# Expert layers: the up matrices of the following pair are issued on ScalarE's own DMA queue instead of SyncE's

## What is computed

```python
SEQ, D_MODEL, N_EXPERTS, TOP_K, D_EXPERT = 256, 1024, 32, 2, 512

def expert_block(args):
    xblk, e = args
    hid = jax.nn.silu(xblk @ w_gate[e]) * (xblk @ w_up[e])
    return hid @ w_down[e]

...
y = jnp.zeros((t, d), xf.dtype).at[sorted_tok].add(contrib)
```

## Time and profile before

| | us |
|---|---|
| median of 3 runs | 2021.74 (2020.07 to 2021.87) |
| profiled execution, its own time | 2024.92 |
| profiled execution, span of the profile | 2023.1 |
| TensorE busy in the span | 1887.4 |
| ScalarE busy in the span | 330.8 |

### The profile page before, as it was taken

How to read it: one execution, slowest core, us unless ns; L and a number is a source line. 1 busy time by engine, 2 the same in 40 slices (tenths; PEclk the granted TensorE clock), 3 DMA queues, 4 the chain that set the end, 5 groups by cost and what they waited for, 6 DMA issues and landing times.

```text
span 2023.1 us, 21197 instructions
## 1 busy us (share of the span) xinstructions
PE 1887.4 (93%) x8074; PEld 958.2 (47%) x8074; DVE 855.9 (42%) x1552; ACT 330.8 (16%) x783; POOL 87.5 (4%) x129
## 2 busy tenths in 40 slices
PE   8999999999999999999999999989999988988886
PEld 4555665455556645855334333333874323332322
DVE  1576898833778887854111111112224111111112
ACT  2452111133521112022001000001002100000000
POOL 4102000001020002000000000000000000000000
PEclk9999999999999999999999999999999999999999
DMA  9315887651168877467999999999346999999995
GB/s 305 96 58 166 308 289 271 235 173 42 58 235 293 294 277 250 135 233 270 365 425 428 428 428 427 428 426 402 130 186 236 417 428 428 428 428 428 427 426 216
DMA packets 149242, 603.14 MB, mean 298 GB/s; under 512 B 16584, under 2 KB 60536, under 8 KB 121232
## 3 DMA queue, kind: packets, MB, share of 16 engines
q1 hardware_dynamic: 144064, 591.43, 74.2%
q0 software_dynamic: 4880, 10.22, 2.0%
q10 hardware_dynamic: 192, 0.05, 0.0%
HBM read 597.67 MB, written 1.10 MB: 296 GB/s over the span
## 4 chain that ended last, share of the span: by engine, by line
PE 63%; DMA 25%; DVE 6%; issue 2%; ACT 2%; DVEq 1%; ACTq 1%; SPq 1%
PE ps L2520 14%; DMA ring<-in_e_w_gate 13%; PE ps L935 12%; DMA ring<-in_e_w_up 11%; PE ps L638 7%; PE ps L1018 5%; PE ps L2350 4%; PE ps L2538 3%; PE ps L2282 3%; PE ps L2365 3%; PE ps L737 2%; PE ps L2464 1%; PE ps L2449 1%; ACTq L1133 1%; DMA ring<-in_e_w_down 1%
## 5 line engine op out<-in xcount | busy, mean ns | idle before, releaser
L2520 PE MATMUL ps<-ring,hT 128*64 128x512 f32 (+1 forms) x1056 | 236.8, 600 | 35.5 <-DMA ring<-in_e_w_gate 17.8
L2538 PE MATMUL ps<-ring,qkT 128*64 128x512 f32 (+1 forms) x1024 | 226.6, 594 | 10.3 <-ACT qkT L2752 8.1
L2520 PE MATMUL ps<-ring,late 128*32 128x512 f32 (+1 forms) x928 | 210.8, 608 | 26.6 <-DMA ring<-in_e_w_up 13.1
L638 PE MATMUL ps<-ring,hT 128*128 128x512 f32 (+1 forms) x384 | 172.0, 593 | 2.7 <-DMA ring<-in_w_in 1.8
L2520 PEld LDWEIGHTS ps<-ring,hT 128*64 128x64 f32 (+1 forms) x1056 | 76.4, 125 | 192.3 <-issue 192.3
L3021 DVE TENSOR_TENSOR qkT<-ps,qkT 128x512 f32<-128x512 f32 (+1 forms) x64 | 44.2, 690 | 256.0 <-PE ps L2538 256.0
L3044 DVE TENSOR_TENSOR qkT<-ps,qkT 128x512 f32<-128x512 f32 (+1 forms) x32 | 22.1, 690 | 299.9 <-PE ps L2520 299.9
L2520 PEld LDWEIGHTS ps<-ring,late 128*32 128x32 f32 (+1 forms) x928 | 68.2, 125 | 164.6 <-issue 164.6
L2538 PEld LDWEIGHTS ps<-ring,qkT 128*64 128x64 f32 (+1 forms) x1024 | 70.9, 123 | 146.5 <-issue 146.5
L1641 DVE SCALAR_TENSOR_TENSOR qkT<-ring,cc,qkT 128x512 f32<-128x512 f32 x168 | 125.8, 749 | 8.6 <-issue 0.4
L3040 DVE TENSOR_TENSOR x<-ps,x 128x1024 f32<-128x1024 f32 x22 | 26.9, 1225 | 193.9 <-PE ps L2449 193.9
(11 more groups left out here) (438 smaller groups left out, 2220.5 us busy)
## 6 DMA issues: line engine op xcount, KB each, us to landing
ring<-in_e_w_down SPq DMA_DIRECT2D x64, 2048.0 KB, 17.0
ring<-in_e_w_up SPq DMA_DIRECT2D x64, 2048.0 KB, 17.3
ring<-in_e_w_gate SPq DMA_DIRECT2D x60, 2048.0 KB, 17.2
ring<-in_ada_w SPq DMA_DIRECT2D x24, 2048.0 KB, 14.0
ring<-in_w_gate SPq DMA_DIRECT2D x16, 1408.0 KB, 8.2
ring<-in_w_up SPq DMA_DIRECT2D x16, 1408.0 KB, 8.6
ring<-in_w_down SPq DMA_DIRECT2D x22, 1024.0 KB, 5.0
ring<-in_w_in SPq DMA_DIRECT2D x8, 2048.0 KB, 11.5
```

What stands on the lines that cost most here:

```text
L638: last = mm(m.ps[:, 4 + i, 0:chunk_width(n)], m.hT[:, j, i * P:(i + 1) * P], w[:, j, :], start=(j == 0), stop=(j == KC - 1))
L2520: last = mm(dst, xg[:, j, at + x * n_tok:at + x * n_tok + place], w(x, j), start=(j == 0), stop=(j == KC - 1))
L2538: lasts[x] = mm(dst, m.hidT[:, j, rows + x * place:rows + (x + 1) * place], half_of(w(x, j), n), start=(j == 0), stop=(j == 3))
```

## The change

SyncE no longer issues the up matrices of the pairs 1 to 15. ScalarE does so, in pair p for pair p + 1, behind the silu and the first share of gather copies and ahead of the wait for the transposes. It waits for the same uses of the same slots as SyncE did. The sizes, slots and semaphores of the loads are what they were, and `second_scalar` now gets the arrays. Pair 0 (and, in further rounds, the up matrices of pair 0) stays with SyncE.

```diff
         def pairs(r):
 
-            pair(r, 1, 1, range(2, N_SLOTS), False)
+            pair(r, 1, 1, (DOWN, DOWN + 1), False)
             with sp.Fori(2, N_PAIRS - 1) as p:
-                pair(r, p, 2, range(N_SLOTS), False)
-            pair(r, N_PAIRS - 1, 2, range(N_SLOTS), True)
+                pair(r, p, 2, (GATE, GATE + 1, DOWN, DOWN + 1), False)
+            pair(r, N_PAIRS - 1, 2, (GATE, GATE + 1, DOWN, DOWN + 1), True)
...
-def second_scalar(nc, act, m):
+def second_scalar(nc, act, m, arrays):
...
                 act.wait_ge(m.e_used[slot_of(p, GATE + 1)], uses_before(r, p, GATE + 1) + 2)
                 a(m.sgx[rows], m.ps[rows, 2, :], ACT.Silu).then_inc(t["esilu"], 1)
                 gathered_next(q, 2 * h)
+                if p + 1 < N_PAIRS:
+                    for f in (UP, UP + 1):
+                        slot = slot_of(p + 1, f)
+                        act.wait_ge(m.e_used[slot], uses_before(r, p + 1, f) + 1)
+                        expert_load(act, m, arrays, l, p + 1, f, by_halves(p + 1), slot).then_inc(m.e_full[slot], 16)
                 act.wait_ge(t["hidT_ps"], it + 1)
```

More of the change, by code:

```diff
@@ L3156, in _ @@
             first_scalar(nc, act, m)
-            second_scalar(nc, act, m)
+            second_scalar(nc, act, m, a)
         @block.tensor
```

## The result

| | before | changed |
|---|---|---|
| median, us | 2021.06 (the runs beside the changed kernel's) | 2059.92 of 4 runs (2056.36 to 2062.72) |
| ratio, 95% | | 1.0189 [1.0174, 1.0204] |
| profiled execution, own time, us | 2024.92 | 2060.24 |
| span, us | 2023.1 | 2058.4 |
| TensorE, ScalarE busy, us | 1887.4, 330.8 | 1897.7, 332.2 |

The changed kernel is slower by 38.9 us, where 19 were forecast: the sign was right, the size half, and 2059.9 lies above the range (2026 to 2055). A stage is counted from its first gate matmul to the end of its last down matmul. The two stages are 36.3 us longer, the rest of the span 1.0 shorter; so all of it lies there. The two profiled executions are 35.3 us apart and not 38.9, because the one of before stood 3.9 us above its median.

The account below looks back on a forecast made before the run. The prediction took the expert layers to be bound by DMA bytes at 428 GB/s; late start 6.9, dry queue 6.0 and stage ends 6 summed to 18.9 us over the 2021.7 us median, forecast 2041 us, range 2026 to 2055.

Parts of the forecast that it names:

- issue time: ScalarE's issuing of up loads, 1.0 us a pair, is hidden or absorbed by load waits: 0, at most 4 us.
- A: Start of expert layer 1: the first up load waits behind the gather copy, so the load stream starts late: +6.9 us.
- B: Expert layer 1, one lap after the start: up lands late and the DMA queue runs dry: +6.0 us.
- A and B, layer 0: Expert layer 0: the late start only eats an existing DMA pause: 0, at most 3 us.
- middle: Middle of both expert layers: bytes unchanged, engines never dry, a pair still costs 29.4 us: 0.
- C: End of each expert layer: up of pair 15 delays gate, leaving TensorE more after the last landing: +3.3, together +6 us.
- By age after all: Rival: hardware serves both queues' loads in order of issue, so little changes: +5.6, 2027 us; chance 0.14.
- equal turns: DMA engines alternate between the two queues, sharing equally for loads with equal rows, rather than serving by age.
- This is just inside 29.4, so 0, but with no room: Expert layer 0, middle: one up-slot lap of 28.9 us fits the 29.4 us pair, so no cost.
- the up slot becomes the bound: Rival: up-slot laps are stretched by TensorE's fallen clock with the queue dry: 12 us more, 2053 us; chance 0.13.
- No difference: Rival: same bytes on same engines, the late start disappears in pauses: 2022 us; chance 0.08.
- Faster: Rival: two queues move more in the expert layers, 445 instead of 428 GB/s: 2009 us; chance 0.07.

Follow-up runs that it names:

- e11: Kernel before, one queue, only pair 1's loads changed: down first, up issued by SyncE behind the gather copies; 2029.2 us, ratio 1.0037.
- e12: Same kernel as e5, measured again on another chip; 2040.7 us, ratio 1.0103 to the kernel before.
- e5: Changed kernel with up loads issued early again: pair 1's by SyncE, the rest by ScalarE directly behind the silu; 2036.7 us, ratio 1.0057.
- e13: e12 plus 8 unread matmuls between the two gate landings of pairs 6, 8, 10, 12, 14 of expert layer 1; 2032.8 us, ratio 1.0054.
- e3: Changed kernel's load order on one queue: SyncE issues all loads, up loads late behind the gather copies; 2031.8 us, ratio 1.0052 to the kernel before.
- e2: Changed kernel with pair 1's up loads back on SyncE as before, the rest late on ScalarE; 2042.1 us, ratio 1.0106 to the kernel before.
- e10: e3 with pair 1's loads as in the kernel before; only up loads of pairs 2 to 15 late; 2023.5 us, ratio 1.0006.
- e4: Changed kernel plus 16 unread matmuls ahead of the gate product of pairs 4, 7, 10, 13 of expert layer 0; 2080.0 us, ratio 1.0309.

## Why the prediction was half right

| term | forecast, us | measured, us | from |
|---|---|---|---|
| issue time | 0 | up to 0.7 a pair; its part of the time not separated | copy L2757 starts 0.9 us after the gather copy does (1584.20, 1583.31), its like before 0.5 (1569.79, 1569.32) |
| A, late start, layer 1 | 6.9 | 6.9 | first load 10.5 us into the stage, 3.7 before |
| B, dry queue | 6.0 | 5.5 | down loads of the pairs 2 to 8 land 12.4 to 12.5 us later into the stage than before, less A; window 1613 to 1619: 2 GB/s |
| A and B, layer 0 | 0 to 3 | 1.9 | landing of pair 4's down loads, from the stage's start |
| middle, both layers | 0 | 15.2 (8.5 and 6.7) | last landing of each stage, less the terms above |
| C, both ends | 6 | 6.9 (3.8 and 3.1) | end of stage less last landing, against before |

**A** held to the tenth as a late start, and the order of the first loads is as forecast. Its price alone is less sure: e11 gives 6.9 to 7.5 us by its times and 4.9 by its trace. **B** held as well: up of pair 1 landed 24.3 us after its issue (23 to 25 forecast), its product started 11.3 us later into the stage than before (12), and the pause came. I had put the issue behind the gather copy and it came at its start, which is 0.5 us. **C** held: expert layer 1 ends 6.9 us behind the last landing (7.1). **By age after all** is refuted by C, by B's pause and by the up load of e12 that overtook a gate load. The Trainium skill (DMA: Bandwidth & Descriptors, "Queues, rings and completion order") has the queues served in turn, and the landings agree. My equal turns were near: ScalarE's queue had 42.5% in the row of e12.

**What failed** is the step "This is just inside 29.4, so 0, but with no room". I had priced one average lap of one slot: gate with one load still to come when up is issued, TensorE at 7.0 us a product, and every lap like the one before. Laps with two queues don't repeat alike. Line L2100 of the changed kernel at two moments, an up load and, 45 us later, a gate load:

```profile
L2100 ACTq DMA_DIRECT2D ring<-in_e_w_up x1: 334/334/334, 1169.1 to 1169.1; - x1
...
DMA to landing us min/median/max: 8.0/8.0/8.0
```

```profile
L2100 SPq DMA_DIRECT2D ring<-in_e_w_gate x1: 333/333/333, 1214.5 to 1214.5; - x1
...
DMA to landing us min/median/max: 24.1/24.1/24.1
```

The first went into idle DMA engines: it took as long as a load into an empty queue, in the middle of a stage that should be full of transfers. The second took 24.1. With one queue loads landed in the order of their issue. With two, up loads issued later are moved while a gate load waits (e12). TensorE then stands still, its clock falls (to a mean of 0.70 to 0.82 of 2.4 GHz over the gate products behind waits of 3.4 to 9.5 us) and the product costs 8.6 to 10.0 us instead of 7.04. The products behind it are all loaded by then and run in one stretch (no wait over 0.2 us from 1147.5 to 1175 us of the changed kernel), so three kinds of slots come free close together and late, and the queues run dry until the next ones do. Two of my signs for the middle fell with this step: up loads landed 8 to 24 us after their issue (14 to 18 forecast), and TensorE waited for up as well, 12 times and 30.9 us in all. That is the rival **the up slot becomes the bound** with its two signs, dry queue and fallen clock, and its 2053 us is the nearest number of the prediction. But it was the gate loads that came late, the up slot only followed, and each late product was stretched by 1.5 to 3.0 us where I had counted 1.7, and the whole came to 15.2 us in place of 12. Against it I had written that "a dry queue only follows if the next load is late too", and 0.13 was too little for a term that I had myself called without room.

**No difference** was the reasoning of the Trainium skill's "Issuing engines are not separate DMA queues" (same page), where issuing from another engine saves sequencer time and no more. For bandwidth the runs agree: no more was moved. But the time did not stay: with nothing changed but the queue it rose by 0.6 and 1.0% (e5, e12), through the order of landing. **Faster** is refuted: with two queues the long windows never reached more than 427 GB/s (e13, expert layer 0), against 428 with one.

The prices don't add up. One queue with all the lateness costs 0.52%, the second queue alone 0.6 to 1.0%, and both together 1.89%. In expert layer 0 that is seen directly: 428 GB/s late on one queue, 423 to 425 on two queues early, 414 to 415 on two queues late (e3; e5, e12; e2, changed). In expert layer 1 the late issue by itself does not make it worse: 456.3 us in e2 against 461.3 in e5. Why the layers differ was not settled; they differ in the rows of a product (64 and 32) and in where gathers stand. What is left in e13 is not slower packets: those of either queue take 0.61 us in the median, as with one queue, and outside the pauses e12 and e13 move 426 to 427 GB/s. So it is pauses too, and which late landing causes which pause was not followed through.

No run beat the kernel before. The nearest, e10, is the same within its interval.

## What to carry to other kernels

When a stage is bound by its bytes and every load is needed in a fixed order, that order is part of the schedule, and a queue keeps it at no cost. Moving one stream to a second queue added no bandwidth here and let loads that are needed later overtake. Before a term is put at 0 because an average lap fits, ask what the worst lap does to the next: here a wait of 3 to 11 us also cost TensorE's clock, and slots that came free in a bunch left the engines dry afterwards. A filler for such a wait must be shorter than the wait, counted in instructions of the trace and not in calls.

## What the runs showed of the hardware

- ScalarE's queue issued the up loads at 1583.31 and 1618.44 us, at the start of the gather copies ahead of them in its program (1583.31 and 1618.43) and not at their end. The two issues together held its queue for 0.84 and 0.82 us, where I had reckoned 1.0, and the next copy started right behind them (1584.20).
- 16 calls of an unread 128x512 float32 matmul are 32 instructions and take 14.0 us, 0.44 us each, at full clock (e4).
- Unread matmuls of 7.1 us in waits of 8 to 11 us made a kernel faster by 7.9 us (e13 beside e12, one chip). The same kind of matmuls, 14.0 us long in waits of 5 us, made one slower by 20 us (e4, 2080.0 us, beside the changed kernel, 2059.9; not measured side by side, ratios 1.0309 and 1.0189).
- Loads of one queue landed in the order of their issue in every kernel; loads of two queues did not: the up load of e12 issued 6.2 us behind a gate load landed 4.7 us ahead of it.
